# An expert layer without its program for 240 columns

## The reference, cut to what matters

```python
def moe_swiglu(h, w_router, w_gate_e, w_up_e, w_down_e):
    xt = h.reshape(-1, d)
    logits = (xt @ w_router).astype(jnp.float32)
    top_val, top_idx = lax.top_k(logits, TOP_K)            # TOP_K = 2
    gates = jax.nn.softmax(top_val, axis=-1)
    order = jnp.argsort(top_idx.reshape(-1))
    xs = xt[order // TOP_K]                                 # frames sorted by expert
    hg = lax.ragged_dot(xs, w_gate_e, sizes)
    hu = lax.ragged_dot(xs, w_up_e, sizes)
    ys = lax.ragged_dot(jax.nn.silu(hg) * hu, w_down_e, sizes)
    out = jnp.zeros_like(xt).at[order // TOP_K].add(ys * gates_in_that_order)
```

## Time and profile before

| | |
|---|---|
| median of 3 launches | 3623.4 us (3622.98 to 3623.42) |
| profiled execution, own time | 3617.46 us |
| its span, first to last instruction | 3615.7 us |
| TensorE matmul busy | 3530.1 us (98%) |
| VectorE busy | 1803.2 us (50%) |
| ScalarE busy | 1539.1 us (43%) |
| GpSimd busy | 205.0 us (6%) |
| mean granted TensorE clock | 0.992 |

### The profile page before, as it was taken

One profiled execution on the slowest core, in us unless ns is written; L12 is line 12 of the kernel. 1 busy time (PEld: TensorE's weight loads), 2 busy tenths in 40 slices (PEclk: granted clock), 3 DMA queues, 4 the chain that ended last, 5 costly groups with the idle time before them and its releaser, 6 DMA issues. The chain is left out here.

```text
span 3615.7 us, 72030 instructions
## 1 busy us (share of the span) xinstructions
PE 3530.1 (98%) x27395; PEld 3362.0 (93%) x27395; DVE 1803.2 (50%) x2599; ACT 1539.1 (43%) x2207; POOL 205.0 (6%) x207
## 2 busy tenths in 40 slices
PE   8999899999999999979999999999999999999997
PEld 7888799999999989879899898998999999999997
DVE  5455553333333554365565565555655545545544
ACT  3455433332332343354454544544545444434433
POOL 1000000000000000040010010100101000100100
PEclk9999999999999999989999999999999999999999
DMA  5111332323222322256565565655655545544543
GB/s 191 37 49 39 135 99 93 99 94 117 93 93 94 123 94 82 89 199 216 185 236 192 195 228 186 234 194 194 220 190 193 188 156 182 189 165 156 183 159 124
DMA packets 158044, 540.83 MB, mean 150 GB/s; under 512 B 23480, under 2 KB 23520, under 8 KB 157920
## 3 DMA queue, kind: packets, MB, share of 16 engines
q1 hardware_dynamic: 129440, 467.72, 39.3%
q0 software_dynamic: 23872, 62.99, 5.0%
q10 hardware_dynamic: 4608, 8.39, 0.6%
HBM read 515.54 MB, written 45.48 MB: 155 GB/s over the span
## 5 line engine op out<-in xcount | busy, mean ns | idle before, releaser
L302 DVE TENSOR_TENSOR wl<-wraw,wh 128x1024 fp32r<-128x1024 f32 x884 | 1082.3, 1225 | 1320.7 <-ACT wh L298 1319.8
L298 ACT ACTIVATE wh<-wraw 128x1024 fp32r<-128x1024 f32 x884 | 934.1, 1057 | 1146.1 <-PE ps L315 1143.8
L315 PE MATMUL ps<-exh,wh 128*128 128x240 f32 (+4 forms) x3595 | 1020.8, 284 | 6.7 <-DVE wl L302 5.9
L315 PE MATMUL ps<-exl,wh 128*128 128x240 f32 (+3 forms) x3584 | 1020.2, 285 | 0.0
L315 PE MATMUL ps<-exh,wl 128*128 128x240 f32 (+3 forms) x3584 | 1019.6, 285 | 0.0
L315 PE MATMUL ps<-xs,wh 128*128 128x256 f32 (+1 forms) x5256 | 827.6, 280 | 2.4 <-DVE qAl L743 2.0
L315 PEld LDWEIGHTS ps<-xs,wh 128*128 128x128 f32 x5256 | 703.1, 189 | 12.5 <-issue 8.7
L315 PEld LDWEIGHTS ps<-exh,wh 128*128 128x128 f32 x3595 | 677.5, 189 | 7.8 <-issue 7.2
L315 PEld LDWEIGHTS ps<-exh,wl 128*128 128x128 f32 x3584 | 677.8, 189 | 0.0
L315 PEld LDWEIGHTS ps<-exl,wh 128*128 128x128 f32 x3584 | 675.9, 189 | 0.0
L315 PE MATMUL ps<-xs,wl 128*128 128x256 f32 x2624 | 516.9, 279 | 0.0
(11 more groups left out here) (318 smaller groups left out, 3518.0 us busy)
## 6 DMA issues: line engine op xcount, KB each, us to landing
wraw<-in_w_expert SPq DMA_DIRECT2D x676, 512.0 KB, 3.3
wraw<-in_w_main SPq DMA_DIRECT2D x208, 512.0 KB, 3.5
hT<-in_xT POOLq DMA_DIRECT2D x2, 2048.0 KB, 9.8
h_d<-hT POOLq DMA_DIRECT2D x2, 2048.0 KB, 10.2
hT<-h_d POOLq DMA_DIRECT2D x2, 2048.0 KB, 13.2
xrow_d<-rows ACTq DMA_DIRECT2D x16, 256.0 KB, 2.0
hrow_d<-rows ACTq DMA_DIRECT2D x16, 256.0 KB, 3.2
yraw<-y_d POOLq DMA_DIRECT2D x4, 768.0 KB, 7.8
```

The source lines that it names most:

```text
L298: act.activation(wh[:, j], wraw[:, j], ACT.Copy).then_inc(hi_done, 1)
L302: dve.tensor_tensor(wl[:, j], wraw[:, j], wh[:, j].bitcast(F32), ALU.subtract).then_inc(lo_done, 1)
L315: mm = pe.matmul(out[:, s], a, b[:, s], start=first and part == 0 and c == 0, stop=last and part == 2 and c + w >= n)
```

## The change

The width 240 is taken out of the tuple. The counts have one width fewer, `by_width` writes one program fewer on each of three engines, and an item with at most 240 tokens runs in the program for 256 columns. The columns past its tokens are computed as well and belong to no token.

```diff
-WIDTHS = (240, 256, 288, 304, 336, CAP)
+WIDTHS = (256, 288, 304, 336, CAP)
```

## The result

The changed kernel's median is 3650.9 us (four launches, 3646.0 to 3652.7) against 3623.2 before: slower, by a ratio of 1.0070 with an interval of 1.0057 to 1.0083. Measured again in a later set it was 3643.7 against 3623.5, ratio 1.0058 (1.0044 to 1.0072). So the change costs 20 to 28 us; the forecast was 24.3. The profiled execution of the first set took 3652.7 us, with a span of 3651.1.

The account below looks back on a forecast made before the run. TensorE's own matmul pace was taken to bound the kernel. Items 0 to 4 at the slow pace gave 5.6 + 6.4 + 6.3 + 6.0 + 0 = +24.3 us, added to the 3623.4 median: 3647.7 us, range 3623.8 to 3650.0.

Parts of the forecast that it names:

- The columns: Items 0 to 2, quick pace: gate and up +1.8 us, down -1.4, so +0.4 or +0.3 an item.
- The pace: Gate and up, items 1 to 4: all slow behind 128-column down stages, +6.4, +6.3, +6.0 and 0 us.
- alternation: Rival for items 0 to 4: slow items hand followers another start; +12.3 or +6.9 us, chance 0.13 together.
- the pace by item: Rival: pace goes with the item, items 0 to 3 quick and item 4 slow; +0.9 us, chance 0.15.
- all quick: Rival: items 0 to 3 quick and item 4 falls into the quick pace too; -5.1 us, chance 0.09.
- Columns paid in full: Rival: gate and up takes time by the column, +8.6 us for each of items 0 to 2; +25.8, chance 0.02.
- Item 0 quick and the others slow: Rival: item 0 adds 0.2 us, items 1 to 3 slow; +18.9 us, 3642.3 us, chance 0.22.
- Down, -1.4 us: Down stage: second token block with 128, not 112, stationary columns is shorter, 79.7 against 81.1 us.
- Item 0, +5.6 us: Item 0: 1200 matmuls behind its hole at the slow pace, 7.0 us, less 1.4 for down.
- the hole that was to hide the first 145 matmuls: Item 0: TensorE stops from 1593.5 to 1599.6 us; resumption stays put, so the matmuls before it cost nothing more.
- The median 5.9 us above the profiled execution: Timed launches may run one more stage slowly than the trace; if item 3, sum 18.3 and time 3641.7 us.
- The removed program, the engines beside: One `fits` instruction fewer, 0.1 us hidden on VectorE; wider work on other engines hidden by TensorE's stream: nothing.

Follow-up runs that it names:

- the pair: Kernel before and changed kernel, both unchanged, profiled again on one chip: span 3622.8 to 3641.7 us, launches 3623.5 and 3643.7 us.
- the 112 run: Changed kernel with 112, not 128, stationary columns in down's second block of tokens in every item of the 256 program: 3629.3 us.
- the run with 128 in the kernel before: Kernel before with 128 stationary columns in both blocks of the 240 program's down stage: 3626.7 us against 3623.2, ratio 1.0008.
- the two runs on the kernel before: Kernel before with gate and up's first matmul whole: 3619.2 us, ratio 1.0001; with no slices at any stage start, layer 0 too: 3630.5 us, ratio 1.0034.

## Why the prediction was right

**The columns.** +0.3 to +0.4 us an item. With the quick pace everywhere, items 1 to 4 of the kernel with 256 columns take 232.0 and 231.9 us against 231.6 with 240: right. The Trainium skill's "TensorE: Matmul & The Clock Gate", "Back-to-back issue gap", has a formula for a single matmul by which 16 more columns are 6.7 ns, an estimate of 9 us an item; these runs show 0.3 to 0.4.

**The pace.** Items 1 to 4 at 238.0 us: predicted to the tenth, and it is nearly the whole cost, +18.8 us of the pair's 18.9. Its reason was half right. The step said that down with blocks of 128 alone hands on the slow pace. What runs showed: the end of down, the way into the loop and the first matmuls of gate and up go with the pace together. By the rule as it stood, item 3 with blocks of 128 in the kernel before and the two kernels with another first matmul would all have been slow, and they were quick. The forecast held because the changed items share with item 4 the way through the loop's back edge, which it named, and the two slices at the start, which it didn't.

| end of the stage before | first matmul | pace | seen in |
|---|---|---|---|
| down with 112, by either way into the loop | two slices | quick | item 3 before; items 1 to 4 of the 112 run |
| down with 128, loop's back edge | two slices | slow | item 4 before; items 1 to 4 after |
| down with 128, out of the 240 loop | two slices | quick | item 3 of the run with 128 in the kernel before |
| down with 112, out of the 240 loop | whole | slow | item 3 of the two runs on the kernel before |
| down with 128, loop's back edge | whole | quick | nine starts; slow in one |
| down with 128, loop's back edge | one more, then slices | quick | four starts |

The table orders what was seen for 256 columns; why these starts give these paces is not shown. Its fifth row has an exception, and layer 0's halves change places between profiles of one program, so the written order alone doesn't fix the pace everywhere.

**The rivals.** With items 1 to 4 all slow, alternation falls (item 2 is slow behind a slow one), and so do the pace by item and all quick. Columns paid in full falls with 231.9 us. Item 0 quick and the others slow is what the second profile of the changed kernel shows; its +18.9 us and the pair's 18.9 agree by chance, since that rival had +0.2 for item 0 and nothing outside the items.

**Down, -1.4 us.** The size held in the items' sum, the cause in part. Blocks of 112 in the 256 program made down 1.4 us longer in all four items (81.1 against 79.7). But with 128 in both blocks, the 240 items' down stage was only 0.5 us shorter, and item 0's first half of down after the change ran at a median of 397 ns with blocks of 128 alone:

```profile
L315 PE MATMUL ps<-wh,mah x56: 397/397/400, 1752.4 to 1790.9; 128*128 128x512 f32 x56
```

So down has more than one pace too, and blocks of 128 alone don't make it the short one.

**Item 0, +5.6 us.** This is the term that was mis-sized: +13.0 in the first profile, -3.2 in the pair from one chip. That the sum of 24.3 lies between the two measured costs, 27.7 and 20.2, is luck in this term. Two of its premises fell. The resumption behind the passage of the clock is slow in the first profile of the changed kernel and quick in the second: it isn't given. And the hole that was to hide the first 145 matmuls isn't there on every chip; where the stretch stands, some 55 matmuls are done by its end, at 1597.9 us in the first profile of the changed kernel.

**The median 5.9 us above the profiled execution.** I suspected one more slow item in the timed launches. The third profile of the kernel before shows all items at their old paces and item 0 at 247.5 and not 239.9 us; on the chip whose profile has the short item 0, launches take 3618.8. So the rows came from an execution without the stretch, and the launches most likely have it, in the kernel before and in the changed one alike. Then it nearly cancels in the difference of the medians, to which the sum was added; the difference of the first two spans, 35.4 us, has it in full. No profile shows item 0 in those launches of the kernel before.

**The removed program, the engines beside.** Nothing in items 1 to 4, as forecast: 238.0 us with the program kept and without it. Items 5 and 6 kept 277.8 and 279.0 us within 0.1. Item 7 didn't: the forecast had nothing for it, and it grew by 0.9 us, through ScalarE's last table load and not through a pace.

The range's upper end, 3650.0, was passed by 0.9 us in the first set and held in the second. It left item 0's own variation out, which these profiles put at 240 to 253 us.

**A version that beats both?** Only in part. Fills ahead of the scatters in the kernel before: 4.5 us less (ratio 0.9988) on a chip without the stretch. The changed kernel with a whole first matmul equals the kernel before (ratio 0.9994) with one program fewer.

## What to carry to other kernels

When two runs of the same program in one trace differ by per cents with no wait in either, compare the matmul records' median in both before you price anything else: a stream can hold one of two paces from its first matmul to its last. An edit that changes what runs just before such a stream, or its first matmul, can then cost or give more than the work it adds, so try the stream's start in two or three forms before you judge the edit. And take a second profile on another chip before a term is sized by one hole.

## What the runs showed of the hardware that I had not expected

- With 128 x 128 stationary and 256 moving columns at full clock, the matmuls start either 113.3 or 117.8 ns apart on average, for a whole stage of some 1340, with records of 276 and 281 ns. One matmul more, or one whole and not in two slices, at the start moved items 1 to 4 from the slow one to the quick one. With 240 columns there are two as well, 112.0 and 113.3 ns.
- On two of the three chips of the experiments, item 0's first units ran with starts up to 2.1 us apart (most of them 0.7 or 1.4) for up to 14 us while GpSimd issued small scatters, with "issue" and not a semaphore as what was waited for, and ScalarE's table load waited 13 to 17 us. The granted clock, 0.71 on average over the 13.7 us of the first changed profile, stood at 0.50 for another 5.6 us behind them, and in the second profile for 2.0 us (1596.6 to 1598.6).
- A table load of ScalarE behind a loop (line 2186 in the kernel before) came 3.4 to 3.7 us after the work before it in the profiles of kernels with the 240 program in the code, used or not, and 4.35 to 4.55 us in those without it.
